# First projections of a hybrid attention layer interleaved with the transposes of x, and the loop over two head groups written out

## What is computed

```
qa, ka, va, qb, kb, vb, ga, gb = split(rms_norm(x, norm_mix_pre) @ w_in)
oa  = sliding-window attention(qa, ka, va) with sinks and a relative bias   # branch A, 8 heads, 2 K/V heads
ob  = stick-breaking attention(qb, kb, vb)                                  # branch B, 8 heads
mix = (sigmoid(ga) * (oa @ w_branch_a) + sigmoid(gb) * (ob @ w_branch_b)) @ w_out
x   = x + rms_norm(mix);  x = x + rms_norm(swiglu(rms_norm(x)))
```

## Time and profile before

| | us |
|---|---|
| median of 3 runs (lowest, highest) | 1669.46 (1668.88, 1671.11) |
| the profiled execution | 1669.05 |
| its span, first to last instruction | 1667.1 |
| TensorE busy in the span | 1592.3 (96%) |
| VectorE, ScalarE, GpSimd busy | 715.4, 604.3, 383.0 |

### The profile page before, as it was taken

One profiled execution on the slowest core, in us unless ns is written; L12 is line 12 of the kernel. 1 busy time (PEld: TensorE's weight loads), 2 busy tenths in 40 slices (PEclk: granted clock), 3 DMA queues, 4 the chain that ended last, 5 costly groups with the idle time before them and its releaser, 6 DMA issues.

```text
span 1667.1 us, 26789 instructions
## 1 busy us (share of the span) xinstructions
PE 1592.3 (96%) x9822; PEld 1459.0 (88%) x9822; DVE 715.4 (43%) x1207; ACT 604.3 (36%) x1279; POOL 383.0 (23%) x263
## 2 busy tenths in 40 slices
PE   6998999999999998899999999999999999999996
PEld 5987988889798897897879898998989989899894
DVE  6363463555736465745452313223132231322318
ACT  6354364464645556534333121212212122121123
POOL 2101102011020110442004331323323233232234
PEclk9999999999999999899999999999999999999998
DMA  6111212121021212445222111111111112111123
GB/s 184 45 57 47 62 40 65 48 66 51 30 68 47 64 43 58 144 142 181 96 80 67 51 50 38 50 38 41 60 38 50 38 38 63 34 54 38 38 102 145
DMA packets 129921, 110.43 MB, mean 66 GB/s; under 512 B 14472, under 2 KB 118192, under 8 KB 129872
## 3 DMA queue, kind: packets, MB, share of 16 engines
q1 hardware_dynamic: 122960, 101.11, 19.6%
q10 hardware_dynamic: 6912, 8.65, 1.5%
HBM read 87.94 MB, written 21.80 MB: 66 GB/s over the span
## 4 chain that ended last, share of the span: by engine, by line
PE 82%; issue 9%; ACT 4%; DVE 3%; DMA 2%; ACTq 1%; POOL 0%; SPq 0%; POOLq 0%
PE m_ya L1496 20%; PE m_yb L1496 10%; PE m_yb L1518 9%; PE b_gm L903 8%; PE a_gm L452 6%; PE a_gm L488 4%; PE m_ya L1518 4%; PE b_gm L925 4%; PE m_ya L1549 3%; PE m_yb L1549 3%; PE b_ob L1020 2%; PE b_zb L977 1%; PE a_ob L553 1%; PE b_tb L1007 1%; ACT b_fail L872 1%
## 5 line engine op out<-in xcount | busy, mean ns | idle before, releaser
L1315 POOL TENSOR_TENSOR w_lo<-f_raw,w_hi 128x1024 fp32r<-128x1024 f32 x66 | 157.8, 2397 | 405.8 <-ACT w_hi L1366 405.8
L1496 PE MATMUL m_ya<-x_hi,w_hi 128*128 128x352 f32 x704 | 227.3, 323 | 1.2 <-DVE x_lo L1631 0.9
L1496 PE MATMUL m_ya<-x_lo,w_hi 128*128 128x352 f32 x704 | 225.6, 320 | 0.0
L1496 PE MATMUL m_ya<-x_hi,w_lo 128*128 128x352 f32 x704 | 225.6, 320 | 0.0
L1366 ACT ACTIVATE w_hi<-f_raw 128x1024 fp32r<-128x1024 f32 x66 | 68.2, 1051 | 213.6 <-PE m_yb L1486 209.3
L1496 PEld LDWEIGHTS m_ya<-x_hi,w_hi 128*128 128x128 f32 x704 | 132.0, 188 | 2.5 <-issue 1.0
L1496 PEld LDWEIGHTS m_ya<-x_hi,w_lo 128*128 128x128 f32 x704 | 132.3, 188 | 0.4
L1496 PEld LDWEIGHTS m_ya<-x_lo,w_hi 128*128 128x128 f32 x704 | 131.9, 187 | 0.0
L800 POOL TENSOR_TENSOR w_lo<-w_raw,w_hi 128x1024 fp32r<-128x1024 f32 x20 | 48.5, 2432 | 341.8 <-ACT w_hi L819 341.8
L1684 DVE TENSOR_TENSOR f_yacc<-m_yb,f_yacc 128x512 f32<-128x512 f32 x132 | 90.9, 690 | 82.0 <-PE m_yb L1518 81.6
L1076 DVE TENSOR_TENSOR_SCAN b_fail<-b_fail 128x128 f32<-128x128 f32 (+8 forms) x72 | 101.1, 1405 | 54.2 <-ACT b_fail L872 54.2
(11 more groups left out here) (248 smaller groups left out, 3838.0 us busy)
## 6 DMA issues: line engine op xcount, KB each, us to landing
f_raw<-in_w_gate_up_dram SPq DMA_DIRECT2D x44, 512.0 KB, 3.9
w_raw<-in_w_in_dram SPq DMA_DIRECT2D x33, 512.0 KB, 3.9
f_raw<-in_w_down_dram SPq DMA_DIRECT2D x22, 512.0 KB, 3.3
m_gate<-gate_scratch SPq DMA_DIRECT2D x16, 528.0 KB, 4.4
gate_scratch<-a_gst ACTq DMA_DIRECT2D x24, 176.0 KB, 1.9
gate_scratch<-b_gst ACTq DMA_DIRECT2D x24, 176.0 KB, 1.8
xtok<-in_x_prompt_dram SPq DMA_DIRECT2D x8, 512.0 KB, 3.4
w_raw<-in_w_out_dram SPq DMA_DIRECT2D x8, 512.0 KB, 4.0
```

The costliest lines, as they stand in the source:

```text
L1315: pool.tensor_tensor(w_lo[:, j % 3, :, :].rearrange("p k n -> p (k n)"), raw[:, j % 2, :], w_hi[:, j % 3, :, :].rearrange("p k n -> p (k n ...
L1496: last = pe.matmul(gm[c][:, 0:CW], w[:, j % 3, k, :], x[:, k, chunk(c)], start=(k == 0 and n == 0), stop=(k == KT - 1 and n == 2))
```

## The change

The loop over the two groups is written out on all five engines: the same instructions for each group with constants in place of registers. For group 0 the projections run chunk by chunk, all three units for one chunk before the next chunk. There each unit has its own bank (`gm_of`), and `done_at` counts them in the new order. TensorE turns tiles 0 to 2, starts on chunk 0, and turns tiles 3 to 8 in between, after the product (unit, chunk, k) that `turn_at` names. ScalarE and VectorE follow orders written out by hand, in which the stacks of chunk 0 stand between the tiles of x. The weights of units 1 and 2 are loaded behind x tiles 2 and 3 (that of unit 0 behind tile 1) and split on ScalarE before tile 3 and tile 4. Unit 3's weight is loaded after the seventh projection of group 0 instead of the third. On VectorE the negated sinks and two memsets of the bias now stand behind all stacks of group 0. Group 1 keeps the order of before. The diff, with parts left out:

```diff
+            def done_at(g, j, c):
+                return c * NPROJ + j if g == 0 else j * NCH + c
+            def order_of(g):
+                return [(j, c) for c in range(NCH) for j in range(NPROJ)] if g == 0 else \
+                       [(j, c) for j in range(NPROJ) for c in range(NCH)]
+            def gm_of(g, j, c):
+                return gm[j] if g == 0 else gm[c]
...
+                def load_kv(g):
+                    for half, at in enumerate((COL_KA + g * HD, COL_VA + g * HD)):
+                        sp.dma_start(w_raw[:, 1, SLOT[2], :, half * HD:(half + 1) * HD], W[:, :, at:at + HD]
+                                     ).then_inc(raw_loaded[SLOT[2]], 16)
...
-                    if t == 2:
+                    if t == 1:
                         load(0, COL_QA)
+                    elif t == 2:
+                        load(1, COL_QA + 2 * HD)
+                    elif t == 3:
+                        load_kv(0)
...
-                with sp.Fori(0, KV_A) as g:
-                    k_at, v_at, c_at = (sp.snap(g * HD + col) for col in (COL_KA, COL_VA, 0))
-                    gate_at = [sp.snap(g * (4 * P) + (COL_GATE + j * P)) for j in range(NU - NPROJ)]
-                    next_at = sp.snap(g * (COL_QB - 4 * HD) + 4 * HD)
-                    sp.wait_ge(gemm_done, past(g * CH))
-                    sp.sem_inc(passed, 1)
-                    load(1, sp.snap(g * (4 * HD) + 2 * HD))
-                    for half, at in enumerate((k_at, v_at)):
-                        sp.dma_start(w_raw[:, 1, SLOT[2], :, half * HD:(half + 1) * HD], W[:, :, bass.ds(at, HD)]
-                                     ).then_inc(raw_loaded[SLOT[2]], 16)
+                for g in range(KV_A):
+                    c_at = g * HD
+                    gate_at = [g * (4 * P) + (COL_GATE + j * P) for j in range(NU - NPROJ)]
+                    if g:
+                        sp.wait_ge(gemm_done, past(g * CH))
+                        sp.sem_inc(passed, 1)
+                        load(1, COL_QA + g * (4 * HD) + 2 * HD)
+                        load_kv(g)
...
-                        sp.wait_ge(gemm_done, past(g * CH + (j + 1) * NCH))
+                        sp.wait_ge(gemm_done, past(g * CH + (done_at(g, j, NCH - 1) + 1)))
...
-                    load(0, next_at)
+                    load(0, COL_QB if g else COL_QA + 4 * HD)
...
-                lo(0, 0)
+                for j in range(NPROJ):
+                    lo(0, j)
...
-                with pool.Fori(0, KV_A) as g:
-                    for j in range(1, NU + 1):
+                for g in range(KV_A):
+                    for j in range(1 if g else NPROJ, NU + 1):
...
-                for t in range(NT + 1):
-                    if t == 3:
-                        hi(0, 0)
...
+                def stack(g, j, c):
+                    act.wait_ge(gemm_done, past(g * CH + (done_at(g, j, c) + 1)))
+                    for a in range(2):
+                        if j < 2:
+                            dst, src = qs[0:HD, 2 * j + a, chunk(c)], gm_of(g, j, c)[a * HD:(a + 1) * HD, 0:CW]
+                        else:
+                            dst, src = kh[a * HD:(a + 1) * HD, chunk(c)], gm_of(g, j, c)[0:HD, 0:CW]
+                        act.activation(dst, src, ACT.Copy).then_inc(stack_hi, 1)
+                measure(0)
+                measure(1)
+                x_parts(0)
+                hi(0, 0)
+                measure(2)
+                x_parts(1)
+                hi(0, 1)
+                x_parts(2)
+                measure(3)
+                hi(0, 2)
+                measure(4)
+                x_parts(3)
+                stack(0, 0, 0)
+                measure(5)
+                x_parts(4)
+                measure(6)
+                x_parts(5)
+                stack(0, 1, 0)
+                measure(7)
+                x_parts(6)
+                measure(8)
+                stack(0, 2, 0)
+                x_parts(7)
+                x_parts(8)
+                for j in range(NPROJ):
+                    stack(0, j, 1)
+                for g in range(KV_A):
+                    if g == 0:
+                        stack(0, 0, 2)
+                        stack(0, 1, 2)
+                        hi(0, 3)
+                        stack(0, 2, 2)
+                        hi(0, 4)
+                        hi(0, 5)
+                    else:
+                        hi(g, 1)
+                        hi(g, 2)
+                        for j in range(NPROJ):
+                            for c in range(NCH):
+                                stack(g, j, c)
+                            hi(g, 3 + j)
...
+                turn(0)
+                turn(1)
+                pe.wait_ge(rel_loaded, 32)
+                pe.matmul(rel_ps[0:H_A, 0:REL], table_sb[:, :], onehot_sb[:, :], start=True, stop=True).then_inc(rel_ready, 1)
+                turn(2)
+                turn_at = {(0, 0, 5): 3, (1, 0, 4): 4, (1, 0, 7): 5, (2, 0, 3): 6, (2, 0, 7): 7, (0, 1, 2): 8}
+                for g in range(KV_A):
+                    for j, c in order_of(g):
+                        if c == 0:
+                            pe.wait_ge(lo_done, past(g * NU + (j + 1)))
+                        if g == 0:
                             if j == 0:
-                                pe.wait_ge(gate_out, past(g * GATES - (c < 2)))
-                            if j == 0:
                                 pe.wait_ge(lo_ready, 2 * -(-(c + 1) * CW // P))
-                            if j:
-                                pe.wait_ge(stack_lo, past(g * ST + (2 * NCH * (j - 1) + 2 * (c + 1))))
-                            for k in range(KT):
-                                for n, (w, x) in enumerate(((w_hi, x_hi), (w_lo, x_hi), (w_hi, x_lo))):
-                                    last = pe.matmul(gm[c][:, 0:CW], w[:, SLOT[j], k, :], x[:, k, chunk(c)],
-                                                     start=(k == 0 and n == 0), stop=(k == KT - 1 and n == 2))
-                            last.then_inc(gemm_done, 1)
+                            if c:
+                                pe.wait_ge(stack_lo, past(2 * (done_at(0, j, c - 1) + 1)))
+                        elif j == 0:
+                            pe.wait_ge(gate_out, past(g * GATES - (c < 2)))
+                        else:
+                            pe.wait_ge(stack_lo, past(g * ST + (2 * NCH * (j - 1) + 2 * (c + 1))))
+                        for k in range(KT):
+                            for n, (w, x) in enumerate(((w_hi, x_hi), (w_lo, x_hi), (w_hi, x_lo))):
+                                last = pe.matmul(gm_of(g, j, c)[:, 0:CW], w[:, SLOT[j], k, :], x[:, k, chunk(c)],
+                                                 start=(k == 0 and n == 0), stop=(k == KT - 1 and n == 2))
+                            if k == KT - 1:
+                                last.then_inc(gemm_done, 1)
+                            if g == 0 and (j, c, k) in turn_at:
+                                turn(turn_at[j, c, k])
...
+                normalise(0)
+                normalise(1)
+                x_parts(0)
+                normalise(2)
+                x_parts(1)
+                dve.wait_ge(rel_ready, 1)
+                dve.tensor_copy(rel_sb[:, :], rel_ps[0:H_A, 0:REL]).then_inc(rel_copied, 1)
+                x_parts(2)
+                normalise(3)
+                normalise(4)
+                x_parts(3)
+                stack(0, 0, 0)
+                normalise(5)
+                x_parts(4)
+                normalise(6)
+                x_parts(5)
+                stack(0, 1, 0)
+                normalise(7)
+                x_parts(6)
+                normalise(8)
+                stack(0, 2, 0)
+                x_parts(7)
+                x_parts(8)
+                for c in range(1, NCH):
+                    for j in range(NPROJ):
+                        stack(0, j, c)
...
-                with dve.Fori(0, KV_A) as g:
...
+                for g in range(KV_A):
+                    if g:
+                        for j, c in order_of(g):
+                            stack(g, j, c)
...
```

More of the change, by code:

```diff
@@ L356, in _ @@
                 act.activation(warm[:, :], epst[:, :], ACT.Sqrt)
-                for t in range(NT + 1):
-                    if t == 3:
-                        hi(0, 0)
[L360 to L391, removed]
+                def measure(t):
+                    r = ROWS[t]
+                    act.wait_ge(x_loaded[t % NX], 16 * (t // NX + 1))
+                    if t:
+                        act.wait_ge(squared, t)
+                    act.activation(junk[0:r, :], xtok[0:r, t % NX, :], ACT.Square,
+                                   accum_out=stat[0:r, t, 0:1]).then_inc(squared, 1)
+                    act.wait_ge(squared, t + 1)
+                    act.activation(stat[0:r, t, 1:2], stat[0:r, t, 0:1], ACT.Sqrt, bias=epst[0:r, 0:1],
+                                   scale=1.0 / D).then_inc(rooted, 1)
@@ new lines, in x_parts @@
```

(36 more changed lines are left out.)

43 lines of the change are left out of this document (9 added, 34 removed).

## The result

| | before | after |
|---|---|---|
| median of the runs (lowest, highest) | 1669.17 (1668.13, 1671.11), 4 runs | 1658.38 (1655.45, 1660.00), 4 runs |
| the profiled execution | 1669.05 | 1660.00 |
| its span | 1667.1 | 1657.2 |

The ratio is 0.9932, interval 0.9914 to 0.995: 10.8 us faster by the medians. The forecast was 1654.8, 14.7 faster, with a range of 1650.5 to 1660.0. The runs after spread over 4.6 us, which the forecast did not allow for. The profiled one is the slowest of the four. A later set of five of the same kernel, on another chip, had its median at 1656.77.

What follows compares the result with a forecast made beforehand. TensorE was taken as the bound, losing time in the head and at the turn of the group loop. 1669.05 - 7.4 - 7.3 = 1654.35, plus 0.4 for the median gave 1654.8; range 1650.5 to 1660.0.

Steps and rivals of the forecast that it cites:

- The turn of the loop: Between groups 0 and 1 on TensorE: written out, the code-fetch gap and low clock behind it go, 7.3 us saved.
- Rivals 3 and 4: 3: the gap between groups isn't the branch's and stays, 1662.1, 8%; 4: branch B's loop is fetched again, 1676.7, 4%.
- Start of the projections: In the head: TensorE's first projection matmul comes at 18.6 us instead of 33.1, after tiles 0 to 2.
- Rival 2: In the head: K and V's weight lands late, at 25, and all later turns slip: 1659.1, chance 10%.
- Rival 1: In the head: TensorE's clock stays low through chunk 0, +11.0 us, 1665.8; chance 6%.
- a sign of being wrong: In the profile after, a low clock past 25 us would show the prediction wrong.
- Edits that cost nothing: Head: moved sinks, memsets, table load and bias round trip, all expected to be covered at no cost.
- VectorE beside POOL: 0 or 0.64 a meeting: Head: a VectorE normalisation meeting GpSimd (POOL) work loses 0 or 0.64 us; allowance ±0.6.
- a cover of 0.7: K and V's third turn: slack of 0.7 us left after moved sinks and memsets delay the first copy about 1.1.
- the forecast's 62.0: End of the head: first gate matmul at 62.0 us instead of 69.4, 7.4 us saved.
- the likeliest case's own range: Whole kernel: the main forecast's own span, 1651 to 1658.5 us; the forecast's chance was 72%.
- So the shift reaches the end: Stages behind the changes: nothing there is fixed in time, so the whole saving shows in the total.

Runs made afterwards that it cites:

- after_again: The changed kernel unaltered, run again on a second chip: median 1656.77, ratio 0.9922 to the kernel before.
- bias_late: Changed kernel with GpSimd's bias copy held until VectorE has written the last x tile's low parts: median 1657.00, ratio 0.9919.
- turn8_late: Changed kernel with TensorE's turn of tile 8 after a third of product (1,1) instead of (0,1): median 1655.40, ratio 0.9919.
- pe_loop_out: Kernel before with the loop over the two groups written out on TensorE alone: median 1662.61, ratio 0.9961.
- b_two_passes: Changed kernel with branch B's loop on TensorE as two turns of two passes each: median 1663.18, ratio 0.996.
- b_written_out: Changed kernel with branch B's loop on TensorE written out, four passes in line: median 1658.32, ratio 0.9934.
- tuned: Changed kernel with late bias copy, later turns 7 and 8, earlier negated sinks and memsets, unit 3's high part before a stack: median 1653.53, ratio 0.9908.
- tuned_warm: tuned plus 58 identity matmuls on TensorE before, between and behind the first three turns: median 1651.92, ratio 0.9896.

## Why the prediction was right, and what its sizes missed

The starts of stages, read from the traces in order of time, give the length of each stage in us. The last column names where the granted clock fell after a pause of TensorE ahead of the merge: T turn 8, G the start of group 1, B the start of branch B.

| profile | first projection | to first gate | group 0's gates, attention | between groups | group 1 | branch B | merge, feed-forward | fell at |
|---|---|---|---|---|---|---|---|---|
| before | 33.1 | 36.3 | 77.5 | 6.0 | 115.4 | 402.4 | 996.4 | G, B |
| after | 18.9 | 48.6 | 77.8 | 0.2 | 113.0 | 401.1 | 997.5 | T |
| after_again | 18.8 | 44.2 | 77.8 | 0.2 | 114.7 | 401.4 | 997.5 | G |
| bias_late | 18.8 | 42.7 | 77.8 | 0.2 | 113.0 | 402.6 | 999.0 | B |
| turn8_late | 18.5 | 43.5 | 77.8 | 0.2 | 113.0 | 403.7 | 996.2 | B |
| pe_loop_out | 32.9 | 35.9 | 77.4 | 0.2 | 113.7 | 402.2 | 996.2 | B |
| b_two_passes | 18.8 | 44.8 | 77.8 | 0.2 | 113.0 | 409.9 | 997.4 | B |
| b_written_out | 19.6 | 45.5 | 77.9 | 0.2 | 113.1 | 402.2 | 996.6 | B |
| tuned | 18.8 | 41.3 | 77.2 | 0.2 | 114.7 | 400.8 | 996.1 | G |
| tuned_warm | 19.7 | 39.8 | 77.2 | 0.2 | 113.0 | 402.3 | 996.0 | B |

**The turn of the loop: right in mechanism and size.** Forecast 7.3 (5.6 of gap, 1.7 of low clock). pe_loop_out takes 5.8 between the groups and 1.7 off group 1, and 7.1 off the median. The changed kernels have another 0.7 less in group 1 (113.0), which no run places. That code is fetched again is shown from both sides: a doubled body stalls (b_two_passes), a written-out one does not (b_written_out), and branch B's plain loop has no transfer of q8. Rivals 3 and 4 did not occur.

**Start of the projections: right.** Forecast 18.6, measured 18.5 to 18.9 where the head's code was the changed kernel's or tuned's, but 19.6 in b_written_out, whose head is the same. There the second tile of x landed later, the first row below; in after_again it is the second row. Why the load took longer stays open. The normalisation that met GpSimd took 1.93, as read in the earlier trace rows. Rival 2 did not occur: ScalarE split K and V's weight by 20.3 in the profile after.

```profile
9.19 1.06 ACT L381 ACTIVATE junk<-xtok 128x1024 f32<-128x1024 f32 x1 [3.22 <-DMA xtok<-in_x_prompt_dram]
...
8.31 1.06 ACT L381 ACTIVATE junk<-xtok 128x1024 f32<-128x1024 f32 x1 [2.79 <-DMA xtok<-in_x_prompt_dram]
```

**The slow stretch behind the start: a little off.** The forecast took over the slow stretch of the kernel before, in which 12 steps between matmuls are of 0.29 and those at its two ends are in between. Of 0.29 there are 17 in the profile after, 8 in after_again, 16 in turn8_late and 10 in tuned. It varies by up to 1.2 us from one profile to the next. Rival 1 did not occur: the clock had risen when turn 3 was done, at 25.2 in the profile after and at 26.0 in b_written_out, although turns stood between the projections. The low clock from 42.4 to 48.4 is past 25, which the prediction had named as a sign of being wrong; it is another fall, behind turn 8's wait.

**Turns and waits.** Turns 3 to 7 took 0.78 to 0.94 each (forecast 0.87). Turn 7 waited 0.41 (0.7), the gates' weight 0.63 (1.0).

**The step that failed** is in "Edits that cost nothing": "The round trip of the bias is issued behind x8, near 34; its copy is due only when the stacks end, at 64." That is true of who needs the copy, and says nothing of when GpSimd makes it. GpSimd had nothing ahead of it and ran it at 38.5, on top of the normalisation for which TensorE was next to wait. The bound "VectorE beside POOL: 0 or 0.64 a meeting" was read from a meeting with a GpSimd instruction that had run for 1.5 us. Its 0.64 is what such a meeting costs when it begins late. In all five meetings with the copy, and in that of the earlier trace rows, the normalisation ends 1.07 to 1.08 after the GpSimd instruction. Here both began together, so it lasted nearly the whole 1.89 and its own time together, 2.90 in all. The forecast had 0.5 for turn 8's wait, measured 1.48 to 1.78 in the four profiles with that meeting and turn 8 in its place. In one of the four the low clock came on top: 20 matmuls at 0.293 instead of 0.159 are 2.7 us, and turn 8 took 0.89 instead of 0.61. The Trainium skill ("SBUF — State Buffer", SBUF: two separate sides) has the rule: the port pair that VectorE and GpSimd share is an exclusive lock, held for the whole instruction, and a VectorE operation with two SBUF inputs takes it against a GpSimd operation that reads SBUF. The traces agree: 2.60 to 2.90 beside the copy of 1.9, and 1.27 with the copy moved.

The same was missed once more, and small: the negated sinks met GpSimd's w_lo at 69.03 and took 2.02 (0.17 in tuned, where they meet nothing), so the third turn of K and V waited 0.38, where a cover of 0.7 had been read.

**The profiled execution adds up so:** the head 5.5 short of the forecast's 62.0: start 0.3, the longer slow stretch with a partly slow turn 3 0.6, turn 8's wait 1.3 and its slow turn 0.4, 20 slow matmuls 2.7, the waits at turn 7 and the gates -0.7, together 4.6. The other 0.9 I can't place singly; between the starts each wait takes some 0.15 more than its idle time. Against the profile before, the stages give -14.2 + 12.3 + 0.3 - 5.8 - 2.4 - 1.3 + 1.2 = -9.9 of span; around the span it has 0.85 more, hence 9.05 faster. In after_again the gates start at 62.92, so that there the head saves 6.5 of the 7.4 forecast; in the first profile it saved 1.9.

**What was luck.** The range reached up to 1660.0 for the sake of rival 2, K and V late, which did not come. The profiled execution took just that, and the median of 1658.38 is just inside the end of the likeliest case's own range (1658.5). What was lost was lost elsewhere, at turn 8 and to the clock behind it. That the first four runs stay inside is in part luck; the later five, at 1656.77, are well inside.

**"So the shift reaches the end" was too simple.** TensorE pauses at turn 8, in the last blocks of a group (waits of up to 0.5 for ScalarE's outputs), at the start of branch B (1.55 before, 1.14 after) and ahead of the merge (6.0). Behind the 6.0 the clock is low in all ten profiles. Each of the first three pauses brought it down in some profiles and not in others, though each of the nine profiles other than before has exactly one such fall: where one place was spared, a later one was not. With nine profiles that is an observation, and no run tests it. At B it fell in before, in bias_late and in five others, and did not in after, after_again and tuned; at G it fell in three profiles and not in seven. Group 1 is 113.0 to 113.7 without the fall and 114.7 to 115.4 with it, branch B 400.8 to 401.4 without and 402.2 to 403.7 with (b_two_passes apart). Before, the fall at G stood behind a gap of 6 us; after, it is one of several that may come without a gap. In after_again it came, and took back the 1.7 us that the forecast had booked. The merge and the feed-forward layer vary by 3 us too, and the two places where their clock sometimes falls (near 756 and 876) don't account for it: turn8_late fell at both and has 996.2. What decides whether a pause brings the clock down stays open. The Trainium skill ("TensorE: Matmul & The Clock Gate", What's actually happening) says that the activity is watched on a free-running count that does not start with the kernel; a fall that comes and goes with the same code and the same wait fits, and no run here tests it.

Why bias_late's head is 6.1 us shorter than in the first profile, and its median no better, follows: against after_again, the execution nearest to the median, its head is 1.5 shorter (61.46 against 62.92), and that is within the spread of the runs.

## What to carry to other kernels

- For an instruction that is moved or left early "because its result is due late", ask when its engine will run it and whom it meets there; if GpSimd and VectorE both work from SBUF, hold the unhurried one back with a wait on work that it would disturb. For a consumer that is close behind its producer, one more product between them takes the wait away, here at no cost that shows.
- Where a hardware loop shows a wait of "issue" at its branch and transfers on the instruction queue, write it out, as here the one of some 1,600 matmuls and weight loads; one that shows neither, as here the one of some 1,400, is to be left alone.
- When one profile of a kernel whose runs spread by 0.2% is compared with another, compare stage by stage, since each may hold another low stretch of the clock.

## What was not expected of the hardware

- A normalisation on VectorE that starts up to 0.4 us behind GpSimd's copy is held back by it: 1.27 becomes 2.60 to 2.90 beside a copy of 1.89, and in each case it ends 1.07 to 1.08 after the copy.
- The same pause of TensorE has two outcomes: after 1.78 us the granted clock was 0.50 for 6 us, after 1.65, 1.64 and 1.48 it stayed at 1.00. In the kernel before the clock fell behind 1.55 at branch B's start as well:

```profile
268.40:273.00 4.60, 4.60 (x19) 4.60 (x20) 0.06 (x1) 1.28 (x1) 0.00 (x0) 0.63 0.35 110
```

- At the projections' start the record grants 1.00 while the matmuls stand 0.293 apart, as in the earlier trace rows; there the spacing tells the clock, not the record.
- A refetched loop of twice branch B's size stalls 5.0 us once at the branch; behind it code arrives in step.
